# Two heads at a time, in the two halves of TensorE's rows, for the scores of a dilated attention; one of its copies on ScalarE; attention sinks as start of the running maxima; an output bias added ahead

## What is computed

```python
def block_attention(q, k, v, blk, n_back, with_prev, sink=None):
    ...
    s = jnp.where(ok[None, :, None, None], s, NEG)
    m = s.max(-1)
    if sink is not None:
        sk = sink.astype(jnp.float32).reshape(1, 1, Hkv, G, 1)
        m = jnp.maximum(m, sk)
    p = jnp.exp(s - m[..., None])
    l = p.sum(-1)
    if sink is not None:
        l = l + jnp.exp(sk - m)
    ...

def mixer_a(x, w_qkv, b_qkv, sinks, w_o, b_o, cos, sin):
    ...
    return o.reshape(B, S, nq).astype(x.dtype) @ w_o + b_o

def mixer_b(x, w_qkv, w_o, cos, sin):
    ...
    for g, (window, dil) in enumerate(B_GROUPS):      # (128, 1), (512, 4), (2048, 16)
        ...
        o, lse = dilated_attention(q, k, qkv[:, :, g, 2], window, dil)
        ...
    w = jax.nn.softmax(jnp.stack(lses), axis=0)
    o = jnp.sum(w[..., None] * jnp.stack(outs), axis=0)

for i in range(DEPTH):                                # in first_block
    ...                                               # h: mixer A, B or C of x
    x = layer_norm(DN_ALPHA * x + h, ln_g[i, 0], ln_b[i, 0])
    x = layer_norm(DN_ALPHA * x + swiglu(x, w_gate_up[i], w_down[i]), ln_g[i, 1], ln_b[i, 1])
```

## Time and profile before

| | |
|---|---|
| median of 3 runs | 2508.11 us (2507.17 to 2510.17) |
| profiled execution, its own time | 2505.91 us |
| its span in the trace | 2503.4 us |
| TensorE / VectorE / ScalarE busy | 97% / 61% / 47% of the span |
| first, second dilated attention, from the products behind the last projection to its last values | 408.96 to 452.54 us, 558.60 to 602.18 us |
| attention of mixer A in layer 0, from its second scores | 61.55 to 89.66 us |
| attention of mixer C, from its second scores | 890.13 to 916.53 us |

### The profile page before, as it was taken

How to read it: one execution, slowest core, us unless ns; L and a number is a source line. 1 busy time by engine, 2 the same in 40 slices (tenths; PEclk the granted TensorE clock), 3 DMA queues, 4 the chain that set the end, 5 groups by cost and what they waited for, 6 DMA issues and landing times.

```text
span 2503.4 us, 30991 instructions
## 1 busy us (share of the span) xinstructions
PE 2429.5 (97%) x12352; PEld 2026.9 (81%) x12352; DVE 1539.1 (61%) x2286; ACT 1173.7 (47%) x1625; POOL 105.9 (4%) x138
## 2 busy tenths in 40 slices
PE   7999999999999999999999999999999999999999
PEld 5788888887888878887788878887888878987887
DVE  6855655546645565457755767676655576686543
ACT  3643354444443464445534444564444355563442
POOL 2100000000000000000100100000100000000000
PEclk9999999999999999999999999999999999999999
DMA  6365343350754427543555334354755334444652
GB/s 237 108 224 201 135 176 127 108 187 27 251 202 157 163 91 249 199 164 144 213 191 202 129 137 169 124 210 144 250 176 194 117 123 181 152 169 164 236 175 88
DMA packets 263117, 418.91 MB, mean 167 GB/s; under 512 B 12192, under 2 KB 149408, under 8 KB 262976
## 3 DMA queue, kind: packets, MB, share of 16 engines
q1 hardware_dynamic: 258112, 400.15, 45.3%
q0 software_dynamic: 4864, 16.80, 1.9%
HBM read 415.86 MB, written 1.05 MB: 167 GB/s over the span
## 4 chain that ended last, share of the span: by engine, by line
PE 86%; DVE 8%; ACT 3%; issue 1%; DMA 1%; POOL 1%; SPq 0%; DVEq 0%; ACTq 0%; POOLq 0%
PE bank_L L1955 39%; PE bank_L L1939 18%; PE bank_S L2149 7%; PE bank_O L2149 7%; PE bank_L L1936 3%; PE bank_O L2088 2%; DVE wlo L1245 2%; PE bank_T L2132 1%; DVE sm L1603 1%; PE bank_S L1939 1%; PE bank_T L2076 1%; ACT whi L957 1%; DVE pts L1626 1%; PE bank_O L1939 1%; PE bank_T L1896 1%
## 5 line engine op out<-in xcount | busy, mean ns | idle before, releaser
L1245 DVE TENSOR_TENSOR wlo<-raw,whi 128x2048 fp32r<-128x2048 f32 (+1 forms) x332 | 712.2, 2169 | 291.8 <-ACT whi L957 291.2
L957 ACT ACTIVATE whi<-raw 128x2048 fp32r<-128x2048 f32 (+1 forms) x332 | 593.7, 1816 | 62.6 <-DMA raw<-in_w_in 20.8
L1955 PE MATMUL bank_L<-whi,xt_hi 128*128 128x512 f32 x1440 | 570.6, 396 | 9.1 <-DVE wlo L1245 7.5
L1955 PE MATMUL bank_L<-wlo,xt_hi 128*128 128x512 f32 x1440 | 562.7, 391 | 0.0
L1955 PE MATMUL bank_L<-whi,xt_lo 128*128 128x512 f32 x1440 | 561.8, 390 | 0.0
L1955 PEld LDWEIGHTS bank_L<-whi,xt_hi 128*128 128x128 f32 x1440 | 271.0, 188 | 65.6 <-issue 9.3
L1955 PEld LDWEIGHTS bank_L<-wlo,xt_hi 128*128 128x128 f32 x1440 | 270.8, 188 | 57.6
L1939 PE MATMUL bank_L<-whi,xt_hi 128*128 128x512 f32 (+1 forms) x800 | 314.2, 393 | 2.9 <-DVE wlo L1245 2.9
L1126 ACT ACTIVATE tok<-bank_L 128x256 f32<-128x256 f32 x132 | 50.7, 384 | 565.2 <-PE bank_L L1955 565.2
L1955 PEld LDWEIGHTS bank_L<-whi,xt_lo 128*128 128x128 f32 x1440 | 271.4, 188 | 53.5
L1939 PE MATMUL bank_L<-wlo,xt_hi 128*128 128x512 f32 (+1 forms) x800 | 308.3, 385 | 0.0
(11 more groups left out here) (311 smaller groups left out, 3235.3 us busy)
## 6 DMA issues: line engine op xcount, KB each, us to landing
raw<-in_w_gate_up SPq DMA_DIRECT2D x176, 512.0 KB, 5.8
raw<-in_w_in SPq DMA_DIRECT2D x72, 1024.0 KB, 5.9
draw<-in_w_down SPq DMA_DIRECT2D x44, 1024.0 KB, 6.1
raw<-in_ffn_w_up SPq DMA_DIRECT2D x88, 512.0 KB, 6.0
raw<-in_b_w_qkv SPq DMA_DIRECT2D x36, 1024.0 KB, 6.9
draw<-in_ffn_w_down SPq DMA_DIRECT2D x22, 1024.0 KB, 6.4
raw<-in_w_lift SPq DMA_DIRECT2D x32, 512.0 KB, 4.5
raw<-in_a_w_qkv SPq DMA_DIRECT2D x12, 1024.0 KB, 8.3
```

The costliest lines, as they stand in the source:

```text
L957: act.activation(wide(whi, w, nkc, ncols)[:, ks, :], wide(raw, w, nkc, ncols)[:, ks, :], ACT.Copy) \
L1245: dve.tensor_tensor(wide(wlo, w, nkc, ncols)[:, ks, :], wide(raw, w, nkc, ncols)[:, ks, :], wide(whi, w, nkc, ncols)[:, ks, :].bitcast(F32 ...
L1955: mm = pe.matmul(banks[bank][:, :], xx[:, k, t * P:(t + 1) * P], ww[:, k, :], start=(k == 0 and q == 0), stop=(k == KC - 1 and q == 2))
```

## The change

**The dilated attention's scores.** Its units are put in a new order: for two neighbouring heads first t = 0 of both, then t = 1 of both. `scores_of_two` is widened to units with several products and several banks, takes all banks of both units first, and issues the products of the two heads alternately.

**One copy on ScalarE.** Of the two copies of a t = 1 unit, the second goes to ScalarE (`copies` in its loop, between the exponentials of unit i and the evacuation of unit i-3). Its semaphore is `pt_act_done`.

**Sinks.** The maximum instructions of mixer A start from the sink, a scalar per row read from `sk8`, rather than from a constant. L1615 is gone.

**Output bias.** A new stage `biased_rows` computes x = ALPHA * x + abo on VectorE, with one instruction of 1024 columns for each of the two tiles, ahead of the last projection of mixer A. `add_residual` then multiplies by 1.0 and has no second instruction.

```diff
@@ attention
-            for u in units:
+            for i, u in enumerate(units):
...
-                n["pt"] += len(u["turns"])
+                u["pta0"], u["by_act"] = n["pta"], [shared and q > 0 for q in range(len(u["turns"]))]
+                n["pta"] += sum(u["by_act"])
+                n["pt"] += len(u["turns"]) - sum(u["by_act"])
+                if in_twos:
+                    seg = u["seg0"] if i % 2 == 0 else seg
+                    u["segs"] = [seg + 2 * b + i % 2 + 1 for b in range(u["banks"])]
...
@@ mixer A
                 add("exp_table")
+                add("biased_rows", inn=n["inn"])
                 tk = next_tok()
@@ mixer B
-                    for h in range(8):
-                        hh = half * 8 + h
-                        for t in range(T):
+                    for pair_ in range(4):
+                        for t, h in [(t, h) for t in range(T) for h in (2 * pair_, 2 * pair_ + 1)]:
+                            hh = half * 8 + h
...
-                    o_is = attention(units, HD ** -0.5, [(aev, n["aev"])], (turn_done, n["turn"]), [st], lead=1)
+                    o_is = attention(units, HD ** -0.5, [(aev, n["aev"])], (turn_done, n["turn"]), [st], lead=1, in_twos=True, shared=True)
@@ ScalarE
+                    def copies(i):
+                        u, k = U[i], at["unit"] + i
+                        for q, (c0, c1) in enumerate(u["turns"]):
+                            if u["by_act"][q]:
+                                if k >= 2:
+                                    act.wait_ge(pv_done, k - 1)
+                                act.wait_ge(tp_done, u["tp0"] + q + 1)
+                                act.activation(pts[:, k % 2, c0:c1], banks[TB[(u["tp0"] + q) % 2]][:, 0:c1 - c0], ACT.Copy) \
+                                   .then_inc(pt_act_done, 1)
...
                             exps(i)
+                        if 2 <= i < len(U) + 2:
+                            copies(i - 2)
                         if i >= 3:
                             evacuate(i - 3)
@@ VectorE
-                ins = dve.scalar_tensor_tensor(out=dst[:, t, cs], in0=x[:, t, cs], scalar=st["alpha"], in1=ps[:, :],
+                ins = dve.scalar_tensor_tensor(out=dst[:, t, cs], in0=x[:, t, cs],
+                                               scalar=1.0 if st["bias"] else st["alpha"], in1=ps[:, :],
                                                op0=ALU.mult, op1=ALU.add)
-                if st["bias"] is not None:
-                    step.did(ins)
-                    step.settle()
-                    ins = dve.tensor_tensor(dst[:, t, cs], dst[:, t, cs], st["bias"][:, cs], ALU.add)
...
+                elif st["kind"] == "biased_rows":
+                    dve.wait_ge(rows_full, 16 * st["inn"])
+                    for t in range(T):
+                        step.did(dve.scalar_tensor_tensor(out=x[:, t, :], in0=x[:, t, :], scalar=ALPHA, in1=abo, op0=ALU.mult,
+                                                          op1=ALU.add))
+                    step.settle()
...
-                                                     scale=1.0, scalar=TAKEN, op0=ALU.add, op1=ALU.max,
+                                                     scale=1.0, scalar=least, op0=ALU.add, op1=ALU.max,
...
-                        if u["sink"]:
-                            j, h = u["sink"]
-                            step.did(dve.tensor_tensor(one, mx, sk8[:, j, h:h + 1].to_broadcast([P, count]), ALU.max))
-                            step.settle()
-                            mx = one
@@ TensorE
+                        two = U[i:i + 2]
+                        name = lambda v, bank: st["qb"][(v["bank0"] + bank) % len(st["qb"])]
+                        for v in two:
+                            for bank in range(v["banks"]):
+                                take(name(v, bank))
+                        for q, pieces in enumerate(zip(*(v["pieces"] for v in two))):
+                            for e in range(len(pieces[0][6])):
+                                for v, (row, off, width, bank, b0, m, products) in zip(two, pieces):
+                                    qq, kk, nk = products[e]
+                                    b1 = b0 + sum(c for _, _, c in products[:e])
+                                    mm = pe.matmul(banks[name(v, bank)][:, b1:b1 + nk], qq, kk, start=True, stop=True)
```

More of the change, by code:

```diff
@@ L190, in build @@
         p_done = sem("p_done")
-        pt_done, rl_done = sem("pt_done"), sem("rl_done")
+        pt_done, pt_act_done, rl_done = sem("pt_done"), sem("pt_act_done"), sem("rl_done")
         pv_done, o_done = sem("pv_done"), sem("o_done")
@@ L244, in finishes, with renorm @@
                 fin[w] = n["lin"]
-        def renorm(norm, dst, alpha, lhs=None, weights=None, bias=None):
+        def renorm(norm, dst, alpha, lhs=None, weights=None, bias=False):
             st = add("renorm", norm=norm, dst=dst, alpha=alpha, lhs=lhs, bias=bias, w=n["w"], gbv=n["gb"],
@@ L329, in headnorm, with attention @@
             return (rope_done, n["rope"])
-        def attention(units, scale, ready, first, behind, lead=2, in_twos=False, fill=(), ps=sm, rounds=0):
+        def attention(units, scale, ready, first, behind, lead=2, in_twos=False, fill=(), ps=sm, rounds=0, shared=False):
             add("attention", units=units, scale=scale, ready=ready, first=first, behind=behind, lead=lead, in_twos=in_twos,
@@ L365, in attention @@
                 n["tp"] += len(u["turns"])
-                n["pt"] += len(u["turns"])
+                u["pta0"], u["by_act"] = n["pta"], [shared and q > 0 for q in range(len(u["turns"]))]
[4 more added lines that the diff above has]
+                    u["segs"] = [seg + 2 * b + i % 2 + 1 for b in range(u["banks"])]
+                else:
+                    u["segs"] = [u["seg0"] + b + 1 for b in range(u["banks"])]
             n["unit"] += len(units)
@@ L557, in build @@
                 add("bound_logs")
-            lhs = renorm("layer", r, ALPHA, lhs, wo, abo if bias else None)
+            lhs = renorm("layer", r, ALPHA, lhs, wo, bias)
             x_is = (x_ready, n["xr"])
@@ L1598, in maxima @@
                         count = len(u["rows"])
+                        least = sk8[:, u["sink"][0], u["sink"][1]:u["sink"][1] + 1] if u["sink"] else TAKEN
                         for q, (row, off, width, bank, b0, m, products) in enumerate(u["pieces"]):
-                            dve.wait_ge(s_done, u["seg0"] + bank + 1)
+                            dve.wait_ge(s_done, u["segs"][bank])
                             shape = (lambda f: f) if len(m.shape) == 2 else \
@@ L1624, in copies @@
                         for q, (c0, c1) in enumerate(u["turns"]):
+                            if u["by_act"][q]:
+                                continue
                             dve.wait_ge(tp_done, u["tp0"] + q + 1)
@@ L2056, in scores_of_two @@
                     def scores_of_two(i):
-                        two = [(v, st["qb"][v["bank0"] % len(st["qb"])]) for v in U[i:i + 2]]
-                        for _, name in two:
-                            take(name)
-                        for q, pieces in enumerate(zip(*(v["pieces"] for v, _ in two))):
-                            for (v, name), (row, off, width, bank, b0, m, products) in zip(two, pieces):
-                                mm = pe.matmul(banks[name][:, b0:b0 + width], products[0][0], products[0][1],
-                                               start=True, stop=True)
-                                if q + 1 == len(v["pieces"]):
-                                    mm.then_inc(s_done, 1)
-                                    held[name] = (ttr_done, v["ttr0"] + q + 1)
+                        two = U[i:i + 2]
[9 more added lines that the diff above has]
+                                    mm = pe.matmul(banks[name(v, bank)][:, b1:b1 + nk], qq, kk, start=True, stop=True)
+                                    if e + 1 == len(products) and (q + 1 == len(v["pieces"]) or v["pieces"][q + 1][3] != bank):
+                                        mm.then_inc(s_done, 1)
+                                        held[name(v, bank)] = (ttr_done, v["ttr0"] + q + 1)
                     def turned(i):
@@ L2077, in turned @@
                             mm.then_inc(tp_done, 1)
-                            held[name] = (pt_done, u["pt0"] + q + 1)
+                            held[name] = (pt_act_done, u["pta0"] + sum(u["by_act"][:q + 1])) if u["by_act"][q] else \
+                                (pt_done, u["pt0"] + q + 1 - sum(u["by_act"][:q + 1]))
                     def values_(i):
@@ L2083, in values_ @@
                         take(name)
-                        pe.wait_ge(pt_done, u["pt0"] + len(u["turns"]))
+                        pe.wait_ge(pt_done, u["pt0"] + len(u["turns"]) - sum(u["by_act"]))
+                        if any(u["by_act"]):
+                            pe.wait_ge(pt_act_done, u["pta0"] + sum(u["by_act"]))
                         c = 0
```

2 lines of the change are left out of this document (1 added, 1 removed).

## The result

The changed kernel takes 2490.43 us (median of 4 runs, 2488.40 to 2493.91), where the kernel before took 2509.14 beside it (4 runs, 2507.17 to 2510.46): a ratio of 0.9928, with a 95% interval of 0.9910 to 0.9945. The forecast was 2490.5. That they agree to 0.1 us is partly luck, as told under the sum.

A forecast was written before the change was run, and what follows sets the result against it. TensorE, busy 97% of the span, was taken as the bound, with VectorE's chain in mixer A. Gains of 15.8 + 1.3 + 0.5 = 17.6 us gave 2490.5 us; likeliest range 2487 to 2494, with neighbouring rivals 2483.5 to 2497.

The forecast's parts named there:

- Part 1, the products: Dilated attention: scores of two heads in different row halves cost 0.87 + 1.50 = 2.37 us instead of 4.70.
- every change of half drains: Rival, chance 0.03: dilated scores run in series and each change of half costs 0.09 us; slower, 2522 us.
- Part 1, the waits: Dilated attention: TensorE waits 0.40 us per two heads for the second T bank and 0.99 once a stage.
- about 0.2 left with the copy on VectorE: Dilated attention: with the moved copy on VectorE, the 0.40 us wait per two heads would be about 0.2.
- VectorE's share rises: Sign expected in the dilated attention: VectorE busy for a larger share of the stage; no size given.
- the sum of 35.9: Dilated stage after the change: scores 8.61, transposes 8.72, values 16.72 - 0.72, waits 0.99 + 4 x 0.40 us.
- Part 2: Sinks in mixer A: period falls from 3.39 to 3.32 us, gaining 1.3 us in two stages.
- Part 3: Bias in the output product: TensorE's wait before the normed rows' transposes vanishes, 0.5 us in two layers.
- The likeliest case: The forecast itself, chance 0.65: 2490.5 us, with its own range of 2487 to 2494.
- TensorE without waits: Rival, chance 0.15: banks released earlier, 10.3 us gained a dilated stage, and the sinks' scalar free; 2483.8 us.
- copies bind: Rival, chance 0.13: slower bank releases, only 5.7 us gained a dilated stage, and nothing from the sinks; 2496 us.
- doesn't pair: Rival, chance 0.04: the halves run one after the other, dilated scores cost 4.70 us again; 2510 us.

The follow-up runs named there:

- the version with both edits: Changed kernel with ScalarE's copies ahead of its exponentials and the sink taken in the negation of the maximum: 2489.16 us, ratio 0.9919 to the kernel before.
- the run alone: Kernel before with only the output bias added to the rows ahead of the product: 2507.63 us, ratio 0.9997.
- both copy runs: Changed kernel with all copies on VectorE, 2490.85 us; changed kernel with ScalarE's copies ahead of its exponentials, 2490.99 us.

## Why the prediction was right

**Part 1, the products.** The 0.87 and 1.50 us for the scores of two heads were measured to the hundredth. The run with heads of one half shows that this is the halves at once. It also shows a gain of the order that I had not set apart: serial scores in the new order cost 4.31, not 4.70. It did no harm, since the sum was built from the paired price. Where the prediction says "the twelve" or counts 24 changes of half per two heads, it took rows for products: there are six products in such a row, and 12 changes. No term of the forecast uses that; only the rival *every change of half drains* would have been 1.1 and not 2.2 us a period, some 2514 and not 2522 us.

**Part 1, the waits.** Forecast: 0.40 us per two heads for the T bank and 0.99 once a stage; period 8.9, stage 35.7. Measured: 0.16 + 0.26 (0.42) and 8.87; once a stage 0.98, counted as the prediction counts (the values start 1.69 us after the six transposes at 409.80, which take 0.71; the 0.82 of the row begins at the transposes' modelled end, 0.87 after their start); stage 35.62. The chain for the second bank was right: from the start of the scores, the copy was to end at 2.89, and ended at 2.84 (423.98 - 421.14). But I had only one bank in it: the first, which VectorE releases, is late too, by 0.16. So "about 0.2 left with the copy on VectorE" was close: the two waits are 0.15 and 0.10 there, and the period 8.70. The sign "VectorE's share rises" says little: it was 65% of the stage and is 66%.

Two smaller steps of it were wrong, in opposite directions. The work without waits is 8.45 us per two heads, not 8.55: transposes that follow values cost 0.33 and 0.66 us, and I had the 0.38 and 0.71 of transposes that follow scores. And the waits at the end of the stage don't vanish: three transposes there last 0.89 until the next ones start (438.78 to 439.67), 0.56 more than the 0.33. By these prices the stage is 32.8 us of work and 2.8 of waits, where the sum of 35.9 had 33.3 and 2.6. The 35.7 was the middle between that sum and a walk that gave 35.5, so its agreement to 0.1 us is partly luck.

The gain was forecast at 7.9 a stage. Of the 7.96 that the stage is shorter, 0.15 is paid ahead of it, by the longer wait of the first scores for ScalarE: 7.8 net, 15.6 in two against 15.8.

**The rule of the Trainium skill**, page "TensorEngine Tiling (Array Packing)", section "Performance Considerations", that PSUM evacuation may become the bottleneck (the page says it of a fourfold speedup of TensorE) and both engines should do it: evacuation doesn't bind here, where the scores became about twice as fast, since VectorE is busy for 27.08 us of 35.12 with all the copies and for 23.49 of 35.62 with a third of them on ScalarE. The advice that follows costs 0.5 us a stage in the order of the change, and gains 0.22 with the copy first (34.90 against 35.12).

**Part 2.** Forecast 3.39 to 3.32, 1.3 us in two (0.07 for each of 16 pairs is 1.1; it was rounded up); measured 3.32 and 0.60 + 0.60 = 1.2. The 0.06 us for a scalar per row, taken from instructions of 1024 columns, holds for 128 columns (0.34 against 0.28) and 256 (0.48 against 0.42), and even for the negation of two numbers in the version with both edits (0.23 against 0.17). In these four sizes it is an amount for each instruction, so it is better paid once a unit than twice.

**Part 3.** Forecast 0.5; measured 0.31 and 0.33 in the changed kernel's layers 0 and 3, and 0.62 in both by the run alone. The wait of the earlier trace rows is gone, and the cover of the earlier trace rows was enough.

**The sum.** 15.6 + 1.2 + 0.6 = 17.4 us against 17.6 by the path. The medians differ by 18.7 in the first comparison and by 17.4 in the last (2509.4, 2492.01). So the mechanism and its size were right, and that the first median is 2490.43 against a forecast of 2490.5 is luck: the kernel before took 1 us more beside it than in the runs that the forecast started from, and the same changed kernel had a median of 2492.01 the second time. The likeliest case was the one that came. *TensorE without waits* falls by the 0.42 and the 0.06; *copies bind* by the period of 8.87, with waits of 0.42 and not 1.0, and by both copy runs; *doesn't pair* and *every change of half drains* by the six paired products in 0.87. The run with one half was worth the run all the same: two heads of one half in that order are what "doesn't pair" describes, and gave 3 us, not the loss I had worked out for it, because I had taken the old price of serial scores (4.70 for 4.31) and put the 0.40 of waits of the paired case on top. Its period of 10.53 us is 4.31 for scores and 6.08 for the rest without waits (8.45 - 2.37), and 0.14 that are left, 0.12 of them waits by the rows above (419.44 is 0.64 and not 0.62 after 418.80, 420.20 is 0.76 and not 0.66 after 419.44). That run has all copies on VectorE, so it is not quite the changed kernel without pairing.

## What to carry to other kernels

Price two row-halves at work from a place in the trace where they already overlap, and then follow the release of every bank, not only of the last one; the work that was taken away had been covering such waits. When an operation is moved to a less busy engine, its place in that engine's row can decide more than the engine's load: behind the exponential it cost 0.5 us a stage, ahead of it it gained 0.2. A gain of 1 to 3 us in 2500 is read from the stages of a profile, because the clock moves the whole by as much.

## Not expected of the hardware

TensorE's granted clock falls from 1.0 to 0.5 (1.2 of 2.4 GHz) in a few short stretches, and not all of them the same in two profiles of the same kernel: the changed kernel has them near 903, 1182 and 2271 us in its first profile, and near 588, 1724 and 2270 in its second. The windows view of the changed kernel, the columns as in the earlier trace rows:

```profile
901.00:902.59 1.59, 0.52 (x5) 0.31 (x4) 1.07 (x2) 0.97 (x2) 0.57 (x2) 1.00 0.46 170
902.59:906.00 3.41, 3.41 (x13) 2.88 (x12) 1.60 (x3) 2.46 (x3) 0.00 (x0) 0.50 0.71 228
1182.48:1189.31 6.83, 6.18 (x23) 5.10 (x24) 2.77 (x4) 4.17 (x6) 1.05 (x2) 0.50 0.48 154
```

The same kernel, profiled again:

```profile
586.00:587.60 1.60, 0.53 (x6) 0.32 (x5) 0.88 (x2) 1.09 (x2) 0.78 (x2) 0.99 0.34 123
587.60:591.00 3.40, 3.40 (x13) 3.03 (x14) 1.87 (x4) 1.23 (x3) 0.00 (x0) 0.50 0.78 251
902.59:906.00 3.41, 3.30 (x18) 2.77 (x19) 1.85 (x3) 2.64 (x3) 0.00 (x0) 1.00 0.81 267
1182.48:1189.31 6.83, 5.76 (x31) 4.61 (x30) 4.38 (x5) 5.78 (x7) 0.46 (x1) 1.00 0.47 154
```

At 902.59 the first profile has half the clock and the second the full one. The falls at 902.59 and at 587.60 both come at a joint where an attention has ended and its output product begins: in the 1.6 us ahead of them TensorE was busy for 0.52 and 0.53 us. That alone doesn't decide it: ahead of 902.59 in the second profile, where the clock stayed full, it was busy for 0.63 of 1.59 us. What the lower clock costs is seen at the first products behind 902.59, in the timeline of TensorE at half clock (first profile):

```profile
903.75 0.78 PE L1976 MATMUL bank_L<-whi,xt_hi 128*128 128x512 f32 x1
904.32 0.63 PE L1976 MATMUL bank_L<-whi,xt_lo 128*128 128x512 f32 x1
```

The same products in the second profile, at full clock:

```profile
903.68 0.48 PE L1976 MATMUL bank_L<-whi,xt_hi 128*128 128x512 f32 x1
903.99 0.39 PE L1976 MATMUL bank_L<-whi,xt_lo 128*128 128x512 f32 x1
```

They start 0.57 us apart at half clock and 0.31 at full, and the second of them lasts 0.63 and 0.39. Each such stretch that I could compare takes 0.8 to 2.4 us from the lead. The profile of the kernel before has one, near 2285 us, beside the last 2 to 4 us of the span, where each profile has one; that of the sinks alone has four, near 613, 920, 1743 and 2289, though its stages are all but those of before. So the pairs aren't needed for them; and they are large enough to hide the 1.0 and 1.4 us by which the copy runs are ahead in their stages, though that they alone keep these out of the medians isn't shown. Over the 21 runs of before the mean clock of a run goes with its span: 2504.1 us at 0.999, a median of 2505.2 at 0.998 (9 runs), 2509.9 at 0.996 (5 runs), 2515.7 at 0.993. The changed kernel's at 0.998 are 2486.6 to 2490.0 (5 runs). Why a stretch comes at one joint and not at another of the same shape stays open; it wasn't tried to keep TensorE at work over a joint.
